# One kernel, one change: the 31-tap convolution for odd and even tokens at once, with channel layouts turned through DRAM and the gate products on GpSimd

## The reference

```python
h = rmsnorm(x, norm_g) * (1.0 + scale[:, None, :]) + shift[:, None, :]
p = h @ w_in                                              # (B, L, IN_COLS)
a_in, a_b, a_c, a_z, b_v, b_g, b_z = jnp.split(p, SPLITS, axis=-1)
y_a = a_b * dwconv(a_c * a_in, conv_a_w) * jax.nn.silu(a_z)          # 3 taps, 512 channels
u = b_v * jax.nn.sigmoid(b_g)
u = dwconv(u, conv_b_w) + conv_b_b                                   # 31 taps, 512 channels
y_b = jax.nn.silu(head_layernorm(u, ln_g, ln_b)) * jax.nn.silu(b_z)  # norm over groups of 64 channels
y = jnp.concatenate([y_a, y_b], axis=-1) @ w_out
return x + gate[:, None, :] * y                                      # then rmsnorm
```

## Time and profile before

| | |
|---|---|
| time, median of 3 runs | 2488.53 us (2488.09 to 2602.07) |
| the profiled execution | 2490.17 us |
| its span on the slowest core, core 1 | 2488.6 us (cores: 2471.5 to 2488.6) |
| mean granted TensorE clock, core 1 | 0.979 of full speed |
| busy: PE, PEld, VectorE, ScalarE, GpSimd | 94%, 41%, 47%, 42%, 21% |
| share of the 16 DMA engines' time, SP's queue | 48.4% |

### The profile page before, as it was taken

How to read it: one execution, slowest core, us unless ns; L and a number is a source line. 1 busy time by engine, 2 the same in 40 slices (tenths; PEclk the granted TensorE clock), 3 DMA queues, 4 the chain that set the end, 5 groups by cost and what they waited for, 6 DMA issues and landing times.

```text
span 2488.6 us, 42355 instructions; the slowest of 8 cores (2471.5 to 2488.6 us)
## 1 busy us (share of the span) xinstructions
PE 2330.9 (94%) x13702; PEld 1028.1 (41%) x13702; DVE 1163.8 (47%) x1859; ACT 1056.7 (42%) x1794; POOL 512.7 (21%) x620
## 2 busy tenths in 40 slices
PE   2899799999999999999999799997999979999797
PEld 0343344444444444444444344443444434444343
DVE  0241654445445544444554445454554554544547
ACT  0224444444544444345444245442454434454334
POOL 5112121122211111222121322122221122221203
PEclk9999899999999999999999899998999989999899
DMA  9944444455444445554444653436553445544444
GB/s 232 201 121 115 143 128 114 128 155 155 122 136 138 128 113 138 155 155 121 138 128 128 181 151 116 144 123 162 155 138 121 143 139 155 154 129 130 144 113 179
DMA packets 283012, 352.63 MB, mean 142 GB/s; under 512 B 152840, under 2 KB 225712, under 8 KB 281776
## 3 DMA queue, kind: packets, MB, share of 16 engines
q1 hardware_dynamic: 275184, 342.59, 48.4%
q0 software_dynamic: 7616, 7.34, 2.2%
HBM read 185.73 MB, written 67.13 MB: 102 GB/s over the span
## 4 chain that ended last, share of the span: by engine, by line
PE 86%; DMA 4%; DVE 3%; SPq 2%; issue 2%; POOL 1%; ACT 0%; DVEq 0%; POOLq 0%; ACTq 0%
PE pb L481 56%; PE pb L668 17%; PE pb L553 8%; DMA xb<-w_out 3%; PE pb L465 2%; PE pb L563 1%; SPq L329 1%; DVE tp L536 1%; PE pb L571 1%; DMA hraw<-xs 1%; POOL w_out_sb L447 1%; DMA yT<-w_ada 1%; SPq L292 0%; DVE tp L533 0%; DVE yT L539 0%
## 5 line engine op out<-in xcount | busy, mean ns | idle before, releaser
L481 PE MATMUL pb<-hT,w_in_sb 128*128 128x512 bf16 x6944 | 1507.2, 380 | 2.2 <-DVE hT L454 2.2
L481 PEld LDWEIGHTS pb<-hT,w_in_sb 128*128 128x128 bf16 x6944 | 680.1, 98 | 824.2 <-issue 7.2
L668 PE MATMUL pb<-w_out_sb,yT 128*128 128x512 bf16 x2048 | 460.6, 381 | 5.5 <-POOL yT L591 3.4
L553 PE MATMUL pb<-X,WC 128*32 128x512 bf16 x4096 | 248.5, 390 | 77.1 <-DVE ga L521 77.1
L668 PEld LDWEIGHTS pb<-w_out_sb,yT 128*128 128x128 bf16 x2048 | 199.6, 98 | 247.1 <-issue 19.0
L631 POOL TENSOR_TENSOR rsE<-msE,mhalf 128x1 f32<-128x1 f32 x128 | 70.2, 548 | 1111.5 <-DVE msE L629 1109.2
L513 DVE TENSOR_TENSOR t<-pb,tp 128x512 bf16<-128x512 f32 x128 | 88.9, 694 | 350.3 <-ACT xs L312 322.9
L519 ACT ACTIVATE tp<-pb 128x512 f32<-128x512 f32 x128 | 76.2, 597 | 412.1 <-DVE tp L536 142.7
L492 DVE SCALAR_TENSOR_TENSOR u<-tp,pb 128x512 bf16<-128x512 f32 x128 | 88.4, 691 | 279.5 <-PE pb L481 260.8
L581 DVE SCALAR_TENSOR_TENSOR pb<-pb,cbs,tp 128x512 f32<-128x512 f32 x128 | 96.8, 756 | 257.4 <-PE pb L571 193.8
L490 ACT ACTIVATE tp<-pb 128x512 f32<-128x512 f32 x128 | 76.1, 597 | 329.6 <-PE pb L481 272.1
(11 more groups left out here) (82 smaller groups left out, 1280.9 us busy)
## 6 DMA issues: line engine op xcount, KB each, us to landing
xb<-x SPq DMA_DIRECT2D x252, 512.0 KB, 6.7
X<-u SPq DMA_DIRECT2D x512, 135.0 KB, 2.9
y<-xb SPq DMA_DIRECT2D x124, 512.0 KB, 3.0
xb<-w_out SPq DMA_DIRECT2D x40, 512.0 KB, 8.2
w_in_sb<-w_in POOLq DMA_DIRECT2D x28, 256.0 KB, 22.1
yT<-w_ada SPq DMA_DIRECT2D x6, 1024.0 KB, 10.1
w_out_sb<-w_ada SPq DMA_DIRECT2D x6, 1024.0 KB, 14.8
xb<-gate_scratch SPq DMA_DIRECT2D x5, 512.0 KB, 6.4
```

The lines of the kernel that those rows point to most:

```text
L481: T.op("tensor", lambda e, bank=bank, kc=kc: e.matmul(bank[:], lhsT=w_in_sb[:, kc, col0:col0 + 128], rhs=hT[:, kc, :], start=(kc == 0), st ...
L553: T.op("tensor", lambda e, q=q, g=g: e.matmul(bank[32 * g:32 * g + 32, :], lhsT=WC[:, j, g, q, :], rhs=X[:, j, g, 4 * q:4 * q + NT], start ...
L668: T.op("tensor", lambda e, bank=bank, kc=kc, sub=sub, h=h: e.matmul(bank[:], lhsT=yT[:, kc, sub * 128:(sub + 1) * 128], rhs=w_out_sb[:, kc ...
```

## The change

The convolution keeps 128 rows of contraction, but as 16 channels by 8 shifts, and its 32 outputs are 16 channels by two phases (odd and even tokens). A tile's 512 tokens are stored as 256 odd ones and then 256 even ones, so each matmul has 256 columns; the number of matmuls stays 128 a tile. For that:

- x is loaded, and y stored, with every other token (`rows`).
- u goes to a DRAM scratch `ud` (`u_out`, two DMAs of 512-byte runs), and `x_fill` reads X from there: 8 DMAs, each into 16 partitions, 512 runs of 536 bytes each. It waits for the tile's `u_out` to land.
- after the convolution the partitions are channels by phases. So the gate gb is turned through DRAM (`g_out`, four DMAs; `g_in`, one), and the product of `ln_out` goes into `yV`, and through DRAM into `yT` (`y_turn`: one store, a wait for it to land, four loads). `y_turn` is issued on SP at j = 3 of `glu`, ahead of `u_out` and `x_fill`.
- bias, gain and Square are different for the two halves of columns, so L565, L581 and L588 become two instructions of 256 columns.
- `conv_a` takes four instructions and a product: its middle tap comes from the same phase and its outer taps from the other. It uses two `TP` buffers.
- `conv_phase` issues the four `conv_b` in a row and moves all of the norm's steps into the hooks of `stage_d`. The ring `sq` has four buffers.
- `fold_gate`: all eight products on GpSimd, loads on GpSimd's own DMA queue into three buffers (two of them in `hraw`), and the steps spread over `glu` j = 2, 3 and `t1_group` j = 0, 1.
- the start: x of tile 0 is loaded right after the first piece of w_ada, its scaling and transposes are issued ahead of the last two pieces; constant blocks are made on VectorE; memsets of u are gone.
- the end: in the last `stage_d` the eight results first take the four products with conv_a's channels, then the others.

```diff
-NQ = 8
+NQ = 4
+HN = NT // 2
+NG = 32
+XW = HN + 4 * (NQ - 1)
...
-        for n in range(4):
+        mod_load(0)
+        a_load(0)
+        for n in range(1, 4):
             mod_load(n)
-        a_load(0)
+        for sub in range(4):
+            a_square(0, sub)
+        a_scale(0)
...
+            if kc == 1:
+                a_transpose(0)
         load_w_in(5, [("yT", 1, 0)])
-        for sub in range(4):
-            a_square(0, sub)
-        a_scale(0)
-        a_transpose(0)
...
+            def load(kc):
+                buf, keys = stg[kc % 3]
+                T.dma("gpsimd", lambda e: e.dma_start(out=buf, in_=wout_d[kc * 128:(kc + 1) * 128, :]),
+                      reads=[], writes=keys + (hkeys if kc < 2 else []), semkey=("fold", kc % 3))
+
+            def step(n):
+                if n == 0:
+                    for kc in range(3):
+                        load(kc)
+                for kc in (2 * n, 2 * n + 1):
+                    buf, keys = stg[kc % 3]
+                    T.op("gpsimd", lambda e, buf=buf, kc=kc: e.tensor_tensor(out=w_out_sb[:, kc, :], in0=buf, in1=gate_bc[:], op=ALU.mult),
+                         reads=keys + [gkey], writes=[("w_out", kc)])
+                    if kc + 3 < 8:
+                        load(kc + 3)
...
+        def u_out(i):
+            udv = ud.rearrange("(j p) h l -> p j h l", p=128)
+            T.dma_batch("sync", [lambda e, h=h: e.dma_start(out=udv[:, :, h, u_base[i]:u_base[i] + HN], in_=u_sb[:, :, h * HN:(h + 1) * HN])
+                                 for h in range(2)], ["u"], [("ud", i)], "st_u")
...
+        def y_turn(i):
+
+            T.dma("sync", lambda e: e.dma_start(out=yd[i % 2], in_=yV[:].rearrange("p j n -> p (j n)")),
+                  reads=["yV"], writes=[("yd", i % 2)], semkey="st_y")
+            src = yd[i % 2].rearrange("(c t) (j hh n) -> hh t c j n", t=2, j=4, hh=2)
+            T.dma_batch("sync", [lambda e, hh=hh, t=t: e.dma_start(out=yT2[i % 2][64 * hh:64 * hh + 64, 4:8, t * HN:(t + 1) * HN], in_=src[hh, t])
+                                 for hh in range(2) for t in range(2)],
+                        [("yd", i % 2)], [("yT", i % 2, 4 + j) for j in range(4)], "ld_y")
...
-            for k in (1, 2):
-                T.op("vector", lambda e, k=k: e.scalar_tensor_tensor(out=acc[:], in0=t1[:, j, k:k + NT], scalar=caT[:, j * KA + k:j * KA + k + 1],
-                                                                   in1=acc[:], op0=ALU.mult, op1=ALU.add),
-                     reads=[("t1", slot), "caT", akey], writes=[akey])
+            T.op("vector", lambda e: e.scalar_tensor_tensor(out=av, in0=right, scalar=w(2), in1=av, op0=ALU.mult, op1=ALU.add),
+                 reads=[("t1", slot), "caT", akey], writes=[akey])
+            for h in range(2):
+                T.op("vector", lambda e, h=h: e.scalar_tensor_tensor(out=out[:, h * HN:(h + 1) * HN], in0=t1[:, j, 1 + h * HN:1 + (h + 1) * HN], scalar=w(1),
+                                                                     in1=acc[:, (1 - h) * HN:(2 - h) * HN], op0=ALU.mult, op1=ALU.add),
+                     reads=[("t1", slot), "caT", akey], writes=[okey])
...
-            fns = [lambda e, g=g, k4=k4: e.dma_start(out=X[32 * k4:32 * k4 + 32, :, g, :], in_=u[32 * g:32 * g + 32, :, k4:k4 + XW])
-                   for g in range(4) for k4 in range(4)]
-            T.dma_batch("sync", fns, [("u", slot)], ["X"], "xfill")
+            fns = [lambda e, w=w: e.dma_start(out=X[16 * w:16 * w + 16], in_=udr[w % 2, :, :, lo + (w + 1) // 2:lo + (w + 1) // 2 + XW])
+                   for w in range(8)]
+            near = [n for n in (i - 1, i, i + 1) if 0 <= n < ntiles and tile_seq[n] == tile_seq[i]]
+            T.dma_batch("sync", fns, ["upad"] + [("ud", n) for n in near], ["X"], "xfill")
...
-            for q in range(NQ):
-                for g in range(4):
-                    T.op("tensor", lambda e, q=q, g=g: e.matmul(
-                        bank[32 * g:32 * g + 32, :], lhsT=WC[:, j, g, q, :], rhs=X[:, j, g, 4 * q:4 * q + NT],
-                        start=(q == 0), stop=(q == NQ - 1), tile_position=(0, 32 * g)),
+            for hh in range(2):
+                for q in range(NQ):
+                    for g in range(4):
+                        G = 8 * j + 4 * hh + g
+                        T.op("tensor", lambda e, q=q, g=g, G=G, hh=hh: e.matmul(
+                            bank[32 * g:32 * g + 32, hh * HN:(hh + 1) * HN], lhsT=WC[:, G * NQ + q].rearrange("p c t -> p (c t)"),
+                            rhs=X[:, G, 4 * q:4 * q + HN], start=(hh == 0 and q == 0), stop=(hh == 1 and q == NQ - 1), tile_position=(0, 32 * g)),
...
+            cs = [conv_b(j) for j in range(4)]
...
+            return {0: norm((ln_center, 0), (ln_center, 1)),
+                    1: norm((ln_center, 2), (ln_var, 0), (ln_rstd, 0)),
+                    2: norm((ln_center, 3), (ln_var, 1), (ln_rstd, 1)),
+                    3: norm((ln_var, 2), (ln_rstd, 2)),
+                    4: norm((ln_var, 3), (ln_rstd, 3))}, (k, cs)
...
+                if j >= 2 and 2 <= i and tile_first[i - 2]:
+                    if j == 2:
+                        fold = fold_gate(tile_seq[i - 2])
+                    fold(j - 2)
...
             if cur_ok:
-                halo(i, u_sb, "u", 15)
+                u_out(i)
...
             if 1 <= i < ntiles:
                 x_fill(i - 1)
+            if 1 <= i <= ntiles:
+                g_in(i - 1)
...
+            if cur_ok:
+                g_out(i)
```

## The result

The changed kernel takes 3027.38 us in the median of 4 runs, against 2489.56 us before. In three of the four one half of the chip ran at a lower clock than the other, as in some runs of every kernel here; the comparison rests on the undisturbed ones, 2971.4, 2972.6 and 2997.5 us against 2488 to 2491 us: a ratio of the means of 1.197, 95% interval 1.188 to 1.207. The forecast was 2362 us.

What follows compares the result with a forecast made beforehand. PE was taken as the bound, without gaps in an ordinary pass. Gains of 69 us (ordinary passes), 46 (folds) and 15 (start), less 3 (end), make 127 off 2488.6: 2362 us, own range 2320 to 2400, about 8 in 10 for 2305 to 2445.

Steps and rivals of the forecast that it cites:

- the convolution: PE's convolution matmuls in each pass: 256 columns instead of 512 take 3.7 us, so the pass loses 3.5 us.
- The first rival: Convolution on PE: weight loads don't run under matmuls, so it gets no shorter; 32 passes lose 3.2 each, 2464 us; 6%.
- The pass it was meant to give: Ordinary pass of the loop: 67.9 us plus 0.9 of jitter, 68.8 instead of 71.45; 26 passes gain 69 us.
- X's rate: Fill of X from DRAM: 2.2 MB into 16 partitions at 105 GB/s takes 21 us.
- the two rows' rules: Length of X's fill: 14 us if the count of runs sets it, 21 if the width in partitions does; width was taken.
- when X is issued: SP's queue: x_fill starts about 25 us into the pass, X complete at about 47, needed at 48.4.
- the second rival: PE waits at the first conv_b for X, landing at 56, 7 late: 2563 us; 10% slower, 8% most gain taken.
- A margin of 1 us: Before the convolution: X complete at about 47, just ahead of 48.4, when PE needs it.
- the transposes: Behind X on SP: landed at about 55, a_modulate 6 us later, just in time; jitter 0.9 us a pass, ends 0 and 5.
- the fold: Five passes with fold_gate on GpSimd: 80.8 us instead of 90.05, a gain of 46 us in all.
- the start: Before the first tile: first a_modulate at about 50 instead of 69.2, a gain of 15 us, ends 5 and 20.
- the end: Last tiles: y_turn exposed for tiles 30 and 31, a loss of 3 us, ends -3 and +8.

Runs made afterwards that it cites:

- e5: Changed kernel with X filled for the first tile only, so its output is wrong: 2554.1 us, ratio 1.025 to the kernel before.
- e11: Changed kernel, X's rows 8 apart, transposes unchained, y loaded behind X, u stored in four pieces, no padding stores, old start: 2512.1 us, ratio 1.0065.
- e1: Changed kernel with X's rows relaid so each fill DMA writes 16 partitions 8 apart: 2863.2 us, ratio 1.148 to the kernel before.
- e9: Changed kernel with the four transposes unchained, none waiting for the one before to land: 2820.3 us, ratio 1.130 to the kernel before.
- e3: Kernel before with the new fold, which also chains its transposes: 2502.2 us, ratio 1.0045.
- e13: Kernel before with its four transposes chained, each waiting for the one before to land, and the old fold: 2542.6 us, ratio 1.021.
- e12: Changed kernel with the twelve padding stores replaced by a memset of X's border columns: 2982.3 us, ratio 1.194 to the kernel before.
- e4: Kernel before with only the new order of the start: 2490.8 us, a single time.
- e16: e11 with the fold pass reordered and the new order of the start: 2476.6 us, ratio 0.9945 to the kernel before.

## Why the prediction was wrong, point by point

**Right: the convolution.** 128 matmuls in 3.68 us where the clock is granted, against 3.7 forecast. The first rival (loads that don't overlap) is refuted. The rule weighed there, the Trainium skill, "TensorE: Matmul & The Clock Gate", "The mechanism", would have made it 7.2 by the prediction's own figure; the trace disagrees. The pass it was meant to give, 68.8 us, is there in e5 (69.06) and e11 (69.05 on core 2, 69.1 to 70.1 in the means of the cores).

**Right: X's rate.** Forecast 105 GB/s and 21 us from the halving with the width; measured 104 to 119. Of the two rows' rules (count of runs, width) e1 decides for the width: same runs, other partitions, 195 GB/s. The Trainium skill, "SBUF — State Buffer", "Door 1: The DMA port swizzle", says it in ports, four for 16 neighbours; the trace agrees, 110 GB/s, and with rows 8 apart 195. By the page these reach eight ports, 218 GB/s as an estimate from its figure.

**Wrong: when X is issued.** The sum had 25 us into the pass, it was 32.5. The two landings ahead of it were taken as 3.0 us from a y store of the kernel before. y took 5.6 from its issue to the next on SP, u 8.6 instead of 4.2. Then X lands at 56.0 instead of 47.5. This is the second rival, "X comes late", almost to the number it named ("at 56, 7 late"; 7.45 measured), but not by its price: it gave 2563, 410 us short of 2972.6, since it held neither the slow clock behind the wait nor what the transposes, the folds, the start and the end cost. It had 10%, with the trace of before speaking "against" it though that trace had no landing in DRAM under such traffic. A margin of 1 us, on three unmeasured lengths in a row, deserved a far larger chance. The Trainium skill, "DMA: Bandwidth & Descriptors", "Anatomy of one DMA — SWDGE (gpsimd) path", puts the fixed 2 us of a DMA on GpSimd's path down mostly to the receipt from the memory that was written, DRAM being the heaviest. Here, on SP's queue, a landing of 0.25 MB in 512-byte runs took 7.9 us at the median; no run here separates the receipt from the transfer.

**Wrong: the transposes.** "Plus `g_in` 1.5, plus 6": they took 20.7, and the first `a_modulate` of the pass began 67 us into it, where 55 was forecast. The step was read from the old queue's row without going through the new dependencies of that very instruction. The consequence was named rightly, `stage_d`'s additions behind a late `a_modulate`, and even as what would make the forecast wrong; but it was priced at 0.9 us with an upper end of 5, and it cost 5.0 and 1.7. e9 shows its size: 152 us.

**Missing: half the clock after a gap.** The first matmuls after each of the long waits run at a granted clock of 0.50, which costs 2.0 us in the convolution and 1.7 in `stage_d`. Over the span, the convolutions' matmuls are busy 174.0 us, where 32 times 3.68 would be 117.8, and those of `stage_d` 525.3, where e11 has 477.6: some 104 us. So a wait of 5 to 8 us costs more than its length; behind one of 1.27 us (e1) the convolution still ran in 3.68.

**Wrong: the fold, in the changed kernel.** Forecast were 80.8 us a fold pass instead of 90.05. The saving itself is real and near the forecast 9.25: 8.6 us where both sides have the chain (e3 and e13). But the chain, unpriced, adds 4.9 us to such a pass (94.1 and 89.2), and in the changed kernel a fold pass costs 18.5 us more than an ordinary one, as before (18.6), where 12 were forecast. The products are 2.35 us, better than the 2.71 taken, but the last one ends 53.1 us into the pass instead of 45.4: a load waits for its buffer each time, the second for the first to land, the first product for the gate. GpSimd's queue was moved past, the halo and `a_scale` behind it with it, and X too: PE waits 24.8 us for it.

**Wrong: the start.** 15 us gained were forecast, 67 lost. The chain costs 27 us up to the third tile in the kernel before (e13), and the first projection came at 84.3 with it and at 60 to 65 without (e9; 63 to 70 before). The twelve padding stores took SP 31 us, unpriced; without them (e12) the third tile came 22 us earlier. And the gain was hardly there to be had, since the second tile's x waits for w_in (e4). The rest is open.

**Wrong: the end.** +3 us was forecast, with ends -3 and +8. From the last tile's first projection on it is 28 us, of which an ordinary pass explains 13; in e16, whose passes are shorter than those before, it is still 18. PE stands for `y_turn` twice, 5.43 and 8.58 us (14.65 and 7.84 in e11), and the 32 matmuls that don't need it cover only a part. No run aimed at this.

The corrections in a row: X's layout and the transposes 303 us together, y's loads 60, u in pieces, padding and old start 98, the fold's order 26, the new start 10 (not shown to be its doing): from 2972.6 to 2476.6, each step a difference of two rows of the table. So the forecast failed in its terms for X's issue, the transposes, the fold, the start and the end, and with all of these corrections the change is worth 0.55%, against the 5% forecast.

## What to carry to other kernels

A margin of about 1 us behind two waits for landings is not a margin: take a landing's length from a row under the traffic that will be there, or leave it as a case with a large chance. When a diff lengthens the list of what a DMA writes, go through every instruction of the batch for the new order among them; waits on SP's own queue show it at once, as a count that is a multiple of the tiles. Where a store to DRAM must land before a read, put other issues between the two, and price the last tile, where there are none to put. And when one part is tried alone, look in its trace for what it brought along and compare it pass by pass: e3's total said that the fold was worth nothing, while its fold passes and its start had moved in opposite directions.

## What the runs showed of the hardware that was not expected

- Padding stores of 16- and 32-byte runs keep the engines busy and move next to nothing: in the changed kernel, 110 to 120 us,

```profile
110.00:120.00 10.00, 9.60 (x44) 4.07 (x43) 2.78 (x4) 0.02 (x1) 0.12 (x1) 1.00 1.09 16
```

  a share of 1.09 at 16 GB/s, and 0.80 at 5 GB/s in the ten us behind.
- Unchanged transfers too took longer to land in the changed kernel, where SP's queue has a share of 73% and not 48%: y stores of 512 KB 3.0 us before, 6.9 after on core 2 (4.9 on core 7); x loads 6.7 and 8.1.
- One long wait of PE halves the pace of what follows: after 7.45 us of standing, the granted clock was 0.50 and 128 convolution matmuls took 5.74 instead of 3.68 us; after 5.04 us, 8 matmuls of 512 columns took 3.57 instead of 1.89. In windows of 20 us this hardly shows (0.98 from 1350 to 1370), in windows of 2 us it does.
- The same bytes in the same 536-byte runs went at 104 to 119 GB/s into 16 neighbouring partitions and at 195 GB/s into 16 that lie 8 apart.
